# Masked attentions of a two-model block kernel: the softmax statistics of two heads taken together

## The reference, cut to what matters

```
# first model, layer 1 ("odd"): 16 heads, 256 tokens + 256 context keys, band mask, a sink per head
s = q @ k.T * SCALE;  s = where(mask, s, NEG_INF)
p = softmax(concat([s, s_context, sink]))[..., :-1]      # the sink only adds to the sum
o = p @ v
# second model, both layers ("second"):
#   8 heads with a chunked window and a sink (SWA)
m = max(max(logits), sink);  e = exp(logits - m);  p = e / (sum(e) + exp(sink - m))
#   4 heads with a forget bias and a causal mask (FoX), 4 heads over selected keys (DSA)
p = softmax(logits)
```

## Time and profile before

| | before |
|---|---|
| time, median of 3 runs | 2448.62 us (2448.02 to 2449.02) |
| profiled execution: span from the first to the last instruction | 2443.0 us |
| PE busy | 2339.1 us (96%) |
| PE weight load busy | 1991.0 us (81%) |
| DVE busy | 1605.4 us (66%) |
| ACT busy | 1156.8 us (47%) |
| DMA: share of 16 engines | 65.4% for the hardware queue |
| chain that ended last | PE 84%, DVE 11%, DMA 2%, issue 2%, ACT 1% |

### The profile page before, as it was taken

How to read it: one execution, slowest core, us unless ns; L and a number is a source line. 1 busy time by engine, 2 the same in 40 slices (tenths; PEclk the granted TensorE clock), 3 DMA queues, 4 the chain that set the end, 5 groups by cost and what they waited for, 6 DMA issues and landing times.

```text
span 2443.0 us, 43518 instructions
## 1 busy us (share of the span) xinstructions
PE 2339.1 (96%) x16455; PEld 1991.0 (81%) x16455; DVE 1605.4 (66%) x3556; ACT 1156.8 (47%) x2149; POOL 0.2 (0%) x4
## 2 busy tenths in 40 slices
PE   7998999999988999999999999999999999999998
PEld 3864678888875699999888899998888899778885
DVE  4567465555476776675676877857667755659893
ACT  3236345444334665645222565543403644458881
POOL 0000000000000000000000000000000000000000
PEclk8998999999999999999999999999899999999999
DMA  9236549999334679765465599546554665469997
GB/s 336 91 111 229 189 133 377 360 377 356 103 96 134 221 221 329 256 180 179 149 207 180 152 309 326 168 147 198 182 173 130 246 211 182 147 219 343 337 358 267
DMA packets 256239, 544.25 MB, mean 223 GB/s; under 512 B 28448, under 2 KB 28704, under 8 KB 255520
## 3 DMA queue, kind: packets, MB, share of 16 engines
q1 hardware_dynamic: 256032, 541.48, 65.4%
HBM read 473.21 MB, written 68.16 MB: 222 GB/s over the span
## 4 chain that ended last, share of the span: by engine, by line
PE 84%; DVE 11%; DMA 2%; issue 2%; ACT 1%; SPq 0%; DVEq 0%; ACTq 0%
PE bank L969 11%; PE bank L973 11%; PE bank L972 11%; PE bank L1332 4%; PE bank L1336 4%; PE bank L1335 4%; PE bank L931 4%; PE bank L1299 2%; PE bank L989 2%; PE bank L1219 2%; PE bank L993 2%; PE bank L992 2%; PE bank L1302 2%; PE bank L1303 2%; PE bank L1506 2%; PE bank L1510 2%
## 5 line engine op out<-in xcount | busy, mean ns | idle before, releaser
L2763 DVE TENSOR_TENSOR WL<-ring,WH 128x512 fp32r<-128x512 f32 x632 | 417.1, 686 | 158.0 <-ACT WH L1936 156.1
L1936 ACT ACTIVATE WH<-ring 128x512 fp32r<-128x512 f32 x632 | 379.6, 624 | 236.4 <-PE bank L969 154.5
L2856 DVE TENSOR_TENSOR WLE<-slots,WHE 128x1024 fp32r<-128x1024 f32 x231 | 281.5, 1224 | 116.3 <-ACT WHE L1936 111.4
L1936 ACT ACTIVATE WHE<-slots 128x1024 fp32r<-128x1024 f32 x231 | 244.8, 1061 | 115.4 <-PE bank L1332 74.5
L969 PE MATMUL bank<-AH,WH 128*128 128x256 f32 (+1 forms) x832 | 267.9, 322 | 8.2 <-DVE AL L2561 4.3
L973 PE MATMUL bank<-AH,WL 128*128 128x256 f32 (+1 forms) x832 | 266.7, 321 | 0.0
L972 PE MATMUL bank<-AL,WH 128*128 128x256 f32 (+1 forms) x832 | 266.7, 320 | 0.0
L969 PEld LDWEIGHTS bank<-AH,WH 128*128 128x128 f32 x832 | 159.5, 192 | 21.2 <-DVE AL L2561 4.9
L972 PEld LDWEIGHTS bank<-AL,WH 128*128 128x128 f32 x832 | 160.5, 193 | 11.2
L973 PEld LDWEIGHTS bank<-AH,WL 128*128 128x128 f32 x832 | 159.3, 191 | 11.2
L969 PE MATMUL bank<-HH,WH 128*128 128x256 f32 (+1 forms) x528 | 166.5, 315 | 0.0
(11 more groups left out here) (449 smaller groups left out, 5720.8 us busy)
## 6 DMA issues: line engine op xcount, KB each, us to landing
ring<-stream SPq DMA_DIRECT2D x864, 256.0 KB, 4.1
slots<-experts SPq DMA_DIRECT2D x264, 512.0 KB, 5.2
WH<-gate_high_parts SPq DMA_DIRECT2D x128, 256.0 KB, 2.9
WL<-gate_low_parts SPq DMA_DIRECT2D x128, 256.0 KB, 3.6
SQ<-stream SPq DMA_DIRECT2D x86, 256.0 KB, 4.5
gate_high_parts<-SQ SPq DMA_DIRECT2D x86, 256.0 KB, 4.1
gate_low_parts<-SQ SPq DMA_DIRECT2D x86, 256.0 KB, 4.8
S<-stream SPq DMA_DIRECT2D x42, 256.0 KB, 4.6
```

The lines of the kernel that those rows point to most:

```text
L1936: return nc.scalar.activation(o, i, fn, **kw)
L2763: V.tensor_tensor(WL[:, s % SPLIT, :], ring[:, c % RING, :], WH[:, s % SPLIT, :].bitcast(F32), ALU.subtract).then_inc(w_taken, 1)
L2856: V.tensor_tensor(WLE[:, s % PAIR_SPLIT, :], pair(pair_of(s)), WHE[:, s % PAIR_SPLIT, :].bitcast(F32), ALU.subtract).then_inc(pair_taken, 1)
```

## The change

The masked attentions leave the loop over units. A pair's two masked maxima now stand one behind the other (`largest_of_pair`), followed by one instruction of two columns for the negated maximum, which raises ACT's semaphore by two. `normalise_pair` adds the sinks and takes the reciprocals of both units in one instruction of two columns each, and then scales the two units one after the other. It works on the pair before, after the maxima of the pair at hand. The even attention keeps the loop. PE's and ACT's instructions stay as they were and in the same order.

```diff
--- before.py
+++ after.py
@@ -2697,7 +2697,45 @@
                     dve.wait_ge(at_o, g0 + p + 1)
                     V.tensor_copy(us[2 * p + 1]["dst"], pv_bank(kind)[:, 0:P]).then_inc(at_out, 1)
 
-                for s in range(len(us)):
+                def largest_of_pair(p):
+
+                    for s in (2 * p, 2 * p + 1):
+                        u, a = us[s], a0 + s
+                        b, c = bank[s % 4][:, 0:u["nk"]], slice(a % 4, a % 4 + 1)
+                        dve.wait_ge(at_s, a + 1)
+                        if s >= 2:
+                            dve.wait_ge(at_e, a - 1)
+                        ins = V.tensor_tensor_reduce(SM[:, a % 2, 0:u["nk"]], b, u["mask"], 1.0, OUT_OF_LIST,
+                                                     ALU.add, ALU.max, mx[:, c])
+                    link(ins)
+                    both, h = slice((a0 + 2 * p) % 4, (a0 + 2 * p) % 4 + 2), us[2 * p]["sink"]
+                    if h is not None:
+                        ins = V.scalar_tensor_tensor(nm[:, both], mx[:, both], -SCALE, nsink[:, h:h + 2], ALU.mult, ALU.min)
+                    else:
+                        ins = V.tensor_scalar(nm[:, both], mx[:, both], -SCALE, None, ALU.mult)
+                    ins.then_inc(at_m, 2)
+
+                def normalise_pair(p):
+
+                    both = slice((a0 + 2 * p) % 4, (a0 + 2 * p) % 4 + 2)
+                    dve.wait_ge(at_e, a0 + 2 * p + 2)
+                    if us[2 * p]["sink"] is not None:
+                        link(V.tensor_tensor(sm[:, both], sm[:, both], es[:, both], ALU.add))
+                    link(V.reciprocal(rc[:, both], sm[:, both]))
+                    for s in (2 * p, 2 * p + 1):
+                        a = a0 + s
+                        e = E[:, a % 4, 0:us[s]["nk"]]
+                        V.tensor_scalar(e, e, rc[:, a % 4:a % 4 + 1], None, ALU.mult).then_inc(at_n, 1)
+
+                for p in range(0 if diff else pairs):
+                    largest_of_pair(p)
+                    if p:
+                        normalise_pair(p - 1)
+                    if p >= 2:
+                        copy_out(p - 2)
+                if not diff:
+                    normalise_pair(pairs - 1)
+                for s in range(len(us) if diff else 0):
                     if diff:
                         if s == 6:
 
@@ -2728,7 +2766,8 @@
                         normalise(s - 1)
                     if s >= 5 and s % 2:
                         copy_out((s - 5) // 2)
-                normalise(len(us) - 1)
+                if diff:
+                    normalise(len(us) - 1)
                 copy_out(pairs - 2)
                 copy_out(pairs - 1)
                 st["a"] += len(us)
```

## The result

| | before | after |
|---|---|---|
| time, median | 2448.82 us (4 runs, 2448.02 to 2449.28) | 2464.80 us (4 runs, 2463.22 to 2472.52) |
| ratio after / before | | 1.009, 95% interval [1.0062, 1.0117] |
| profiled execution: span | 2443.0 us | 2461.5 us (its own time 2463.22 us) |
| DVE busy | 1605.4 us | 1582.3 us |
| odd attention, first scores to the product behind it (L989) | 78.5 us | 96.6 us |

What follows compares the result with a forecast made beforehand. PE, waiting on DVE's stretch from first maximum to first scaling, bounds the kernel: 15.5 odd + 7.2 SWA + 1.6 DSA + 0 FoX + 3 clock = 27.3 us, giving 2476 us; own range 2468 to 2484, wide range 2463 to 2490.

Steps and rivals of the forecast that it cites:

- The bound and the chain: Whole span: chain 84% PE, 11% DVE; the 20.5 us of DVE work removed runs beside PE and gains nothing.
- rival 2: Odd and SWA attentions: DVE's queue holds PE, so less DVE work saves 20.5 us, about 2428 us; chance 0.04.
- Rival 4: Whole kernel: ACT or the weight stream gives the time back later, within 5 us of 2449; chance 0.03.
- The turn: Odd attention: second maximum and even scaling delay PE's value products, 1.14 us more a turn, 5.70 instead of 4.56.
- How many turns: Odd attention: thirteen turns give 14.8 us, short first turns 0.4, tail 0.3; 15.5 us, bounds 14 to 18.
- The clock: Odd attention: PE's longer idling lowers its granted clock three times at about 1 us, 3 us; likeliest at step 8.
- rival 1: Odd attention: clock falls become the habit, 8 or more, 35 us in all, about 2484 us; chance 0.12.
- SWA: Both SWA attentions: PE waits 0.53 or 0.38 us in seven steps each; 7.2 us with restarts, bounds 4 and 9.
- Rival 3: Second model: gate products hide the longer DVE stretch, only the odd attention pays, about 2467 us; chance 0.07.
- DSA and FoX: Second model: DSA waits 0.28 and 0.13 us, two steps of each per layer, 1.6 us; FoX 0, at most 1.
- The sum: Whole kernel: 27.3 us on the span of 2443.0, plus 5.6 us by which runs exceed it, about 2476 us.

Runs made afterwards that it cites:

- e3: Kernel before with the change's order (both maxima, then both scalings of the pair before) but small instructions not merged; 2501.06 us, ratio 1.0226.
- e1: Changed kernel with pairs in the odd attention only, second model unit by unit as before; 2462.92 us, ratio 1.0075 to the kernel before.
- e7: Kernel before with the odd unit's scaling moved ahead of the wait for scores, in the odd attention only; 2438.76 us, ratio 0.9983.
- e2: Changed kernel with pairs in the second model's attentions only, odd attention unit by unit as before; 2447.55 us, ratio 1.0009 to the kernel before.
- e5: Kernel before with the odd unit's scaling moved ahead of the wait for scores in all masked attentions; 2441.09 and 2437.40 us, ratios 0.9989 and 0.9975.

## Why the prediction was right

**The bound and the chain.** Right. The chain in the odd attention is PE's three lines and DVE's, and the rest of DVE's work is beside it. 23.1 us of DVE work went (20.5 forecast) and brought nothing: rival 2, a gain of up to 20.5 us, fell. In the same order merging saves 0.45 us a turn (e3 against the change). The Trainium skill, "VectorE: DVE Perf Modes", section on the errata of SBUF-source instructions, has a fixed cost for each instruction, so that fewer and wider ones are better; with the order kept, the traces agree with it by these 0.45 us. Rival 4, that later stages give the time back, fell too: the stretch behind the odd attention is 296.0 us in both traces of the changed kernel and 297.2 in that one of the kernel before which has their pace, so at most 1.2 us come back there.

**The turn.** Right. 5.70 forecast, 5.63 measured. By its terms: first maximum 0.61 (0.62), fetch 0.00 (0.08; the second maximum starts with the fetch), second maximum 0.62 (0.62), fetch to the negated maximum 0.19 (0.12), small ones 0.46 (0.51), scaling to transposes 0.55 (0.54), transposes 1.02 (1.03). The bounds for the fetch, 0.08 to 0.12, did not hold it; the effect is 0.08 us a turn.

**How many turns.** Mis-sized, in both directions. I counted 13 turns at 1.14 us and put 0.4 on the start and 0.3 on the tail. The trace has 15 places where the pair's maxima stand ahead of a scaling: the turn behind the first one went from 4.31 to 5.62, and the last one pays as well: the stretch from the last scores to the products behind the attention grew by 1.4 us, 0.3 more than a turn does, as forecast for the tail. 13 turns at 1.07 give 13.9, the start 1.3, the end 1.4: 16.6 us, for 15.5 forecast. With the clock, 1.5, it is 18.1 us. A steady turn counted between its first and last anchor leaves out both ends of the loop, which pay as well.

**The clock.** 3 us forecast in all, 1.5 measured in the odd attention, at step 8 as named. In the other turns PE idles 1.48 of 5.63 us and the clock stays at 1.00, so rival 1 (the habit) did not come; e3, 0.45 us a turn longer, has it. The place came out as named, but the length of the idle time does not explain it alone: ahead of the transposes of the first pair PE idles 2.49 us, no less than at step 8, and the clock did not fall there. In the FoX and DSA attentions there are falls in the kernel before as well, and their number changes between executions: each of these stages took 35.6 to 41.8 us in the two traces of the kernel before, and 39.7 to 44.3 in the two of the changed one. For both stages together, e1 and e7, which go unit by unit there, give 78.9 and 72.7 us beside the 75.7 and 82.0 of the kernel before, and e2, which goes by pairs, 84.1 beside the 82.5 and 85.3 of the changed one. All three by pairs lie above all four others, by 6.6 us in the mean. Against a loss of that size stand the runs of e2, whose interval ends at 7.1 us in all, 6.8 of which the SWA attentions take. Whether the change adds falls of the clock there is open.

**SWA.** 7.2 us forecast, 6.4 measured (3.2 each). Seven waits in each attention, as forecast, of 0.30 to 0.32 and of 0.17 to 0.18 us in the brackets, less than the 0.4 to 0.5 that I wrote there; the first kind is 0.47 us of delay by the starts, for a forecast of 0.53. Rival 3, which had the gate products hide this, fell.

**DSA and FoX.** Two waits of 0.11 us in each layer's DSA and none in FoX: below the 1.6 us forecast for DSA, and 0 for FoX was right.

**The sum.** 18.1 + 6.4 + about 0.5 = 25.0 us, for 27.3. Errors of the terms cancel in part: the odd attention without its clock was 1.1 us too low, and the clock 1.5, SWA 0.8 and DSA 1.1 too high. The forecast time, 2476 us, was 11.2 us above the first median. 2.3 us of this are the terms. 3.9 are the 5.6 us that I put around the span: the changed kernel's execution had 1.7 us around it, the copy of the kernel before 1.9 (2437.90 and 2436.0 us); the median of other executions was no measure of that. The remaining 5.0 are what is left of the 6.5 by which the two first spans lie closer together than 25.0, through the pace of the feed-forward parts and the clock outside the odd attention, of which I took none into account, when the 1.6 by which the median lies above the profiled execution are taken off. So 2464.80 us lies 3.2 us below the forecast's own range (2468 to 2484) and nearer to rival 3 (2467) than to 2476; that it still lies in the wide one, whose lower end is 2463, by 1.8 us, is luck, since a pace and falls of the clock of which I knew nothing moved it by more. The time alone could not tell the forecast from rival 3. What tells them apart is that L1252 waits in SWA, and that the odd attention alone (e1) brings 18.5 of the 24.5 us.

## What to carry to other kernels

Before merging small instructions of two items, write down which item the awaited engine wants first: the merge makes the early one wait for the late one, and a large instruction that slips ahead with it costs its full length in every turn. Count such a cost for each pass of the loop, the first and the last too. If an engine idles just ahead of the critical stretch, the cheap gain is to move the awaited instruction into that gap (0.39 us a turn here), not to shorten what runs beside the bound.

## What the runs showed of the hardware

- One stream of matmuls with their weight loads (128x256, PE never idle, granted clock 1.00) runs at 113 or at 117 to 118 ns each, for 150 us and longer, and in two executions of one kernel the slow pace stands in different parts (e5), or in one part and then in none of the two shown (the kernel before). In the first trace of the kernel before it holds from about 880 to 1100 us and makes that part about 7 us longer. What chooses it is open; the DMA share is high at either (0.96 to 0.99), so the rows name no cause.
- Executions of the kernel before that were compared here range from 2429 to 2460 us. The first four happened to lie within 1.3 us; a spread from few runs is no measure of what a comparison can resolve.
- A masked maximum behind another starts with the fetch of the first one's result, 0.61 us after it for 512 columns, not behind it.
- PE's clock stayed at 1.00 with 1.48 us idle in every 5.63 us. It fell after the idle time of 2.46 us at step 8, in both executions and in e1, but not after one of 2.49 us at the first transposes. In e3, with 1.58 us ahead of the transposes in every 6.08 us, it fell seven times in one attention. No single length of idle time tells these apart.
